# Two chained transformer blocks in one kernel: FFN products with the tokens stationary, 1/rms moved behind the products, token tiles staggered across stage borders

## The chip, the cores and the metric

The kernel runs on one core of a Trainium2 chip. The metric is the device time of one execution in microseconds, median over repeated runs. A profile is taken from one execution; its span runs from the first to the last instruction. Engines: PE (TensorE, matmul), PEld (its weight load), DVE (VectorE), ACT (ScalarE), POOL (GpSimd), SP (SyncE, here the queue that issues most DMAs).

## What is computed

The input is `x` of 256 tokens by 1024, in float32. Two layers of a first block and two of a second act on it. A block of the first kind is, per layer,

```python
h = rms_norm(x, ffn1_norm[l])
x = x + 0.5 * swiglu(h, ffn1_w_gate[l], ffn1_w_up[l], ffn1_w_down[l])
h = rms_norm(x, mix_norm[l])
... = split_in_proj(h @ w_in[l])       # four attentions side by side, 16 heads
x = x + o @ w_out[l]
h = rms_norm(x, ffn2_norm[l])
x = x + 0.5 * swiglu(h, ffn2_w_gate[l], ffn2_w_up[l], ffn2_w_down[l])
```

with `rms_norm(x, g) = x * rsqrt(mean(x*x) + eps) * g` and `swiglu(h, wg, wu, wd) = (silu(h @ wg) * (h @ wu)) @ wd`, 2816 hidden columns. A block of the second kind scales and shifts each normed input by rows that come from a 1024-vector `c` (`mod = silu(c) @ w_ada[l] + b_ada[l]`), mixes, norms the mixer's and the FFN's output again (`x + gate * rmsnorm(y, g_post)`), and has one FFN per layer.

```python
h = rmsnorm(x, g_ffn_pre[l]) * (1.0 + scale_f) + shift_f
x = x + gate_f * rmsnorm(swiglu_2(h, w_gate_up[l], w_down[l]), g_ffn_post[l])
```

## The kernel before

**Stages.** `STAGES` lists ten: f0 a0 f1 f2 a1 f3 b0 f4 b1 f5 (f an FFN, a a mixer of the first block, b one of the second). All engines go through them in the same order, each in its own program; semaphores are the only ties. X (256 x 1024) stays in SBUF as two token tiles t = 0, 1 of 128 partitions.

**Split products.** All large products are float32 made of two reduced parts: each operand is a high half (a rounded copy, tiles `Wh`, `Hh`, `PTh`) and a low half, the remainder (`Wl`, `Hl`, `PTl`). A product is three matmuls, high x high, high x low, low x high (`three`, lines 404 to 406; in the FFN lines 474 to 476).

**Weights.** They come as pieces of 128 x 1024 (512 KB) in the order of use: SP loads into six `raw` tiles, ACT writes the high half (line 791), DVE the remainder (line 1088), into rings of six `Wh` and `Wl`. In the programs `hi_to(n)` and `lo_to(n)` say how far the conversion goes at that point; ACT then waits in line for the raw tile and for the ring slot (`w_used`).

**Norm.** At each stage's start, `norm` in four programs: ACT squares X and sums (line 800); POOL takes the power -1/2 (lines 1554, 1556); PE turns X by eight transposes of 128 x 128 per tile (line 421) and spreads 1/rms over the partitions by small matmuls (line 426); DVE multiplies turned X, gain and 1/rms into `HT` (a part of `WK`, line 1132), ACT writes `Hh` (line 808 or 810) and DVE `Hl` (line 1124 or 1126), chunk by chunk of 128 columns of the model width, both tiles together.

**FFN** (`ffn`). For each of 22 groups f of 128 hidden columns: the gate and up weights are the stationary side, the turned tokens `Hh`, `Hl` move, 256 columns; 48 matmuls. ACT takes silu (line 827), DVE the product with up (line 1162), ACT and DVE split it (lines 831, 1164) into `PTh`, `PTl`, which already lie with hidden columns on partitions. The down product of group f - 1 follows: `PTh` stationary, the down weights move, 512 columns, 12 matmuls, accumulating in PSUM banks 0 to 3 over the whole stage. In f0 to f3 DVE also makes the rows of `w_ada` ("ada steps", line 1152, fed by ACT's DMAs into `BT`), with a small matmul, a row addition and a DMA out per eight steps.

**Mixers.** `project` has the tokens stationary and 512 weight columns moving (lines 404 to 406). Mixer a follows `walk_a`, which weaves projections, head norms, rotations, transposes and the 20 attention items; mixer b has 16 items. `out_proj` takes the eight output pieces one by one, both token tiles with each.

**Stage end.** `residual` on DVE (line 1192) adds the four banks to X, first tile 0, then tile 1; in stages b0 to f5 `post_norm` does it with squares on ACT (line 1050), POOL's power and two wide DVE operations (lines 1201, 1205). Then `norm` of the next stage begins.

## Time and profile before

| | us |
|---|---|
| median of 3 runs | 1968.66 (1967.34 to 1969.95) |
| the profiled execution's own time | 1968.9 |
| its span | 1967.0 |
| PE busy | 1752.2 (89% of the span) |
| DVE busy | 1292.5 (66%) |
| ACT busy | 900.1 (46%) |
| POOL busy | 105.8 (5%) |

The page counts 27994 instructions, 10912 of them matmuls. Busy time of PE is read with care: matmuls overlap, so the start-to-start distance in the timeline says what one costs in a stream. "Granted clock" is TensorE's clock as a share of its full speed.

### The profile page before, as it was taken

To read this page: it belongs to the slowest core of one execution; us is meant where nothing else is said; L and a number is where in the kernel's file an instruction comes from. 1 tells how busy PE (TensorE), PEld (TensorE's weight loads), DVE (VectorE), ACT (ScalarE), POOL (GpSimd) and SP (SyncE) were. 2 spreads that over 40 slices of the span, in tenths; PEclk is the share of its full clock that TensorE was granted. 3 is DMA by queue.
4 is the path that set the end of the run, shared out by engine and by line. 5 is a ranking of instruction groups with operands and counts; after the bars stand their busy time and mean duration, and the time that the engine had idled before them with its cause. 6 is when DMAs were issued, how large, how long until landed. Compare 5 with 4: busy or idle time off the path is not lost.

```text
span 1967.0 us, 27994 instructions
## 1 busy us (share of the span) xinstructions
PE 1752.2 (89%) x10912; PEld 1577.7 (80%) x10912; DVE 1292.5 (66%) x2143; ACT 900.1 (46%) x1577; POOL 105.8 (5%) x141
## 2 busy tenths in 40 slices
PE   6999976789999999986689999977899987779998
PEld 5999765579998999865579998866799976669997
DVE  5776668667776777668757776585555556754554
ACT  4444534444444444544434445464444455634443
POOL 0000012000000000011100000011000000200000
PEclk9999987699999999988589999968899988779999
DMA  7777522047775877632137875403355652134552
GB/s 266 263 258 233 203 90 82 22 158 251 261 240 183 270 264 239 211 107 77 31 118 250 273 247 174 147 1 118 140 184 183 182 162 81 63 105 155 191 182 89
DMA packets 99698, 332.01 MB, mean 169 GB/s; under 512 B 18624, under 2 KB 18880, under 8 KB 99056
## 3 DMA queue, kind: packets, MB, share of 16 engines
q1 hardware_dynamic: 84928, 277.84, 42.9%
q10 hardware_dynamic: 14640, 52.39, 7.6%
q8 instruction: 87, 1.43, 0.3%
q14 instruction: 43, 0.35, 0.1%
HBM read 329.09 MB, written 1.10 MB: 168 GB/s over the span
## 4 chain that ended last, share of the span: by engine, by line
PE 76%; DVE 13%; ACT 5%; issue 3%; POOL 2%; DMA 1%; ACTq 0%; DVEq 0%; POOLq 0%
PE PS L474 13%; PE PS L475 13%; PE PS L476 13%; PE PS L404 10%; PE PS L405 10%; PE PS L406 10%; DVE Wl L1088 2%; ACT Wh L791 1%; ACT WK L860 1%; PE PS L547 1%; DVE st L1222 1%; DVE WK L1219 1%; PE PS L528 1%; POOL A L1587 1%; PE PS L662 1%
## 5 line engine op out<-in xcount | busy, mean ns | idle before, releaser
L1088 DVE TENSOR_TENSOR Wl<-raw,Wh 128x1024 fp32r<-128x1024 f32 (+2 forms) x514 | 605.1, 1217 | 234.5 <-ACT Wh L791 233.7
L474 PE MATMUL PS<-Hh,Wh 128*128 128x256 f32 x2112 | 605.7, 287 | 14.1 <-DVE Hl L1124 9.0
L475 PE MATMUL PS<-Hl,Wh 128*128 128x256 f32 x2112 | 601.4, 285 | 0.0
L476 PE MATMUL PS<-Hh,Wl 128*128 128x256 f32 x2112 | 600.9, 285 | 0.0
L791 ACT ACTIVATE Wh<-raw 128x1024 fp32r<-128x1024 f32 (+2 forms) x514 | 509.1, 1036 | 113.5 <-DVE GQ L1174 61.2
L474 PEld LDWEIGHTS PS<-Hh,Wh 128*128 128x128 f32 x2112 | 407.5, 193 | 23.9 <-DVE WK L1132 14.7
L475 PEld LDWEIGHTS PS<-Hl,Wh 128*128 128x128 f32 x2112 | 409.1, 194 | 4.7
L476 PEld LDWEIGHTS PS<-Hh,Wl 128*128 128x128 f32 x2112 | 408.9, 194 | 0.0
L827 ACT ACTIVATE WK<-PS 128x256 f32<-128x256 f32 x132 | 50.7, 384 | 446.8 <-PE PS L476 446.8
L404 PE MATMUL PS<-Wh,Hh 128*128 128x512 f32 (+2 forms) x472 | 194.3, 412 | 24.3 <-DVE Hl L1474 6.2
L404 PE MATMUL PS<-Wh,PTh 128*128 128x512 f32 x528 | 207.2, 392 | 0.0
L405 PE MATMUL PS<-Wl,PTh 128*128 128x512 f32 x528 | 207.1, 392 | 0.0
L406 PE MATMUL PS<-Wh,PTl 128*128 128x512 f32 x528 | 205.3, 389 | 0.0
L405 PE MATMUL PS<-Wl,Hh 128*128 128x512 f32 (+2 forms) x472 | 190.2, 403 | 0.0
L406 PE MATMUL PS<-Wh,Hl 128*128 128x512 f32 (+2 forms) x472 | 188.9, 400 | 0.0
L1162 DVE TENSOR_TENSOR WK<-WK,PS 128x256 f32<-128x256 f32 x132 | 55.2, 419 | 189.0 <-ACT WK L827 188.5
L1152 DVE SCALAR_TENSOR_TENSOR GQ<-BT,cact,GQ 128x512 f32<-128x512 f32 x168 | 126.1, 751 | 21.7 <-DMA BT<-in_ada 14.6
L404 PEld LDWEIGHTS PS<-Wh,Hh 128*128 128x128 f32 x472 | 96.9, 205 | 47.1 <-issue 27.1
L406 PEld LDWEIGHTS PS<-Wh,PTl 128*128 128x128 f32 x528 | 99.2, 188 | 21.9
L404 PEld LDWEIGHTS PS<-Wh,PTh 128*128 128x128 f32 x528 | 99.5, 189 | 18.7
L547 PE MATMUL PS<-CT,WK 128*128 128x128 f32 x224 | 53.3, 363 | 68.2 <-POOL WK L1570 40.7
L405 PEld LDWEIGHTS PS<-Wl,PTh 128*128 128x128 f32 x528 | 99.5, 188 | 16.9
(191 smaller groups left out, 1872.3 us busy)
## 6 DMA issues: line engine op xcount, KB each, us to landing
raw<-in_ffn SPq DMA_DIRECT2D x396, 512.0 KB, 4.6
BT<-in_ada ACTq DMA_DIRECT2D x96, 512.0 KB, 4.4
raw<-in_win SPq DMA_DIRECT2D x64, 512.0 KB, 4.5
raw<-in_wo SPq DMA_DIRECT2D x32, 512.0 KB, 4.0
raw<-in_win SPq DMA_DIRECT2D x8, 420.0 KB, 4.0
BT<-in_nab SPq DMA_DIRECT2D x2, 1024.0 KB, 9.5
...
```

What stands on the lines that cost most here:

```text
L404: e.matmul(out_, xh, wh, start=start, stop=False)
L405: e.matmul(out_, xh, wl, start=False, stop=False)
L406: return e.matmul(out_, xl, wh, start=False, stop=stop)
L474: e.matmul(o, h[:, cc], Hh[:, c, :], start=c == 0, stop=False)
L475: e.matmul(o, h[:, cc], Hl[:, c, :], start=False, stop=False)
L476: ins = e.matmul(o, lo[:, cc], Hh[:, c, :], start=False, stop=c == 7)
L547: ins = e.transpose(PS[:, 5 + z % 2, col:col + 128], src, ident)
L791: e.activation(Wh[p % RING][:, 0:w], raw[p % RAW][:, 0:w], ACT.Copy).then_inc(w_hi, 1)
L827: e.activation(SB[:, f % 2, 0, :], PS[:, 4 + f % 2, 0:S], ACT.Silu).then_inc(f_silu, 1)
L1088: e.tensor_tensor(Wl[p % RING][:, 0:w], raw[p % RAW][:, 0:w], Wh[p % RING][:, 0:w].bitcast(f32), ALU.subtract).then_inc(w_lo, 1)
L1152: e.scalar_tensor_tensor(out=acc, in0=w, scalar=cact[:, c:c + 1], in1=acc, op0=ALU.mult, op1=ALU.add).then_inc(ada_step, 1)
L1162: e.tensor_tensor(SB[:, f % 2, 1, :], SB[:, f % 2, 0, :], PS[:, 4 + f % 2, S:2 * S], ALU.mult).then_inc(f_mul, 1)
```

## The change

**FFN.** A group is now 256 hidden columns (`NG` = 11), one token tile at a time. The turned tokens are the stationary side and a piece of gate and up weights moves: 256 gate and 256 up columns side by side, 512 in one PSUM bank (`gate_up`, banks 4 and 5 in turn). The host lays the weights out to match. The product `silu(gate) * up` then has tokens on partitions (`FA`, three buffers in `WK`), so PE turns it (`turn`, two transposes per group and tile, banks 6 and 7, shared with the ada rows) before ACT and DVE split it into `ATh`, `ATl` (four buffers in the memory of `PTh`, `PTl`). `down` is as before, per tile.

**1/rms.** In stages f0 to f3, a0 and a1 X is turned unscaled; the gain rides on the copy out of PSUM, and 1/rms (`rms(s, t)`, per token, which is now a partition) rides on the silu, the up product and the copies of the projections. In b and later FFNs a shift has to be added, so DVE first scales X by 1/rms into a spare tile (`scale_x`). The spreading matmuls are gone. ACT copies half of the turned chunks into `XT` and DVE the other half, 128 x 128 each, before the split.

**Order.** One function `walk(s)` gives each stage's events in order, and all engines follow it. `("gu", g, t, 0)` is gate/up of group g for tile t, `("down", g, t, chunks)`, `("turn", g, t, 0)` as above, `("res", s, t, 0)` the residual and the squares of tile t, `("turn_x", s, t, h)` the turning and splitting of half h of tile t for stage s, `("xs", ...)` the scaling. Tile 0 ends its stage early and is turned for the next one (`nxt`) while tile 1 still has products; tile 1 is turned (`mid`) after the next stage's first products of tile 0. `out_proj` gives its last pieces tile by tile.

**Weights.** Four more slots lie in the memory of `QTh`, `QTl` in FFNs and around them (`MORE`). `last_use`, `freed` and `slot_free` say when a piece's slot is free; `weights(s, i)` stands ahead of every event on ACT and DVE and converts up to `weights_to[s, i]`: what the event needs, plus at most `LIMIT` pieces whose slot is already free.

```diff
-NF = F // 128
+NG = F // 256
-RAW, RING = 6, 6
+RAW, RING, MORE = 6, 6, 4
+def walk(s):
+    kind, k = STAGES[s]
+    late = s >= 6
+    mid = [("turn_x", s, 1, 0), ("turn_x", s, 1, 1)]
+    nxt = [("turn_x", s + 1, 0, 0), ("turn_x", s + 1, 0, 1)] if s + 1 < len(STAGES) else [None, None]
+    scale = [[("xs", s + 1, t, 0)] if s + 1 in range(6, len(STAGES)) else [] for t in range(2)]
+    nlate = s + 1 >= 6
+    ev = []
+    if s == 0:
+        ev += [("turn_x", 0, t, h) for t in range(2) for h in range(2)]
+    if kind == "f":
+        def round_(g):
+            got = [("gu", g, 0, 0)]
+            if g:
+                got += [("turn", g - 1, 1, 0), ("down", g - 1, 0, (0, 1))]
+            got += [("gu", g, 1, 0), ("turn", g, 0, 0)]
+            if g:
+                got += [("down", g - 1, 1, (0, 1))]
+            return got
+        if s == 0:
+            ev += round_(0) + round_(1)
+        else:
+            ev += [("gu", 0, 0, 0), *(() if late else mid), ("gu", 1, 0, 0), *(mid if late else ()), ("gu", 0, 1, 0),
+                   ("turn", 0, 0, 0), ("gu", 1, 1, 0), ("turn", 0, 1, 0), ("down", 0, 0, (0, 1)), ("turn", 1, 0, 0),
+                   ("down", 0, 1, (0, 1))]
+        for g in range(2, NG - 2):
+            ev += round_(g)
+        y, z = NG - 2, NG - 1
+        ev += [("gu", y, 0, 0), ("turn", y - 1, 1, 0), ("down", y - 1, 0, (0, 1)), ("gu", z, 0, 0), ("turn", y, 0, 0),
+               ("down", y - 1, 1, (0, 1)), ("gu", y, 1, 0), ("turn", z, 0, 0), ("down", y, 0, (0, 1)), ("down", z, 0, (0, 1)),
+               ("turn", y, 1, 0), ("res", s, 0, 0), ("gu", z, 1, 0), *scale[0]]
+        if nlate:
+            ev += [("down", y, 1, (0,)), ("turn", z, 1, 0), ("down", y, 1, (1,)), ("down", z, 1, (0, 1)), *nxt]
+        else:
+            ev += [nxt[0], ("down", y, 1, (0,)), ("turn", z, 1, 0), ("down", y, 1, (1,)), nxt[1], ("down", z, 1, (0, 1))]
+    elif kind == "a":
+        ev += [("proj", 0, 0, 0), *mid, ("proj", 1, 0, 0), ("proj", 0, 1, 0), ("norm", 0, 0, 0), ("proj", 1, 1, 0), ("rope", 0, 0, 0),
...
+               *(("att", i, 0, 0) for i in range(10, ITEMS["a"] + 3)), ("mix", 0, 0, 0),
+               ("wo", (0,), 0, 0), ("wo", (0,), 1, 0), ("sums", 0, 0, 0), ("wo", (1,), 0, 0), ("wo", (1,), 1, 0),
+               ("wo", (2,), 0, 0), ("wo", (2,), 1, 0), ("rows", 0, 0, 0), ("wo", (3,), 0, 0), ("wo", (3,), 1, 0),
+               ("wo", (4,), 0, 0), ("wo", (4,), 1, 0), ("wo", (5, 6, 7), 0, 0), ("res", s, 0, 0), *scale[0],
+               ("wo", (5, 6), 1, 0), nxt[0], ("wo", (7,), 1, 0), nxt[1]]
+    else:
+        ev += [("proj", 0, 0, 0), ("proj", 1, 0, 0), *mid, ("proj", 0, 1, 0), ("proj", 1, 1, 0), ("proj", 2, 0, 0), ("proj", 2, 1, 0),
+               ("bulk", 0, 0, 0), ("proj", 3, 0, 0), ("proj", 3, 1, 0), ("lat", 0, 0, 0),
+               *(("att", i, 0, 0) for i in range(-1, ITEMS["b"] + 3)), ("mix", 0, 0, 0),
+               ("wo", (0,), 0, 0), ("wo", (0,), 1, 0), ("wo", (1,), 0, 0), ("wo", (1,), 1, 0),
+               ("wo", (2, 3, 4, 5, 6, 7), 0, 0), ("res", s, 0, 0), *scale[0], ("wo", (2, 3, 4, 5, 6, 7), 1, 0), *nxt]
+    ev += [("res", s, 1, 0), *scale[1]]
+    return [e for e in ev if e]
...
+        for p in range(NP):
+            s = stage_of[p]
+            wide = STAGES[s][0] == "f" or p < first[STAGES[s]] + 8
+            if p == first[STAGES[s]] and s and STAGES[s - 1][0] != "f":
+                for n in range(RING, RING + MORE):
+                    holder[n] = freed[wo_at[STAGES[s - 1]]] + 1
+            slots = range(RING + MORE if wide else RING)
+            slot_of[p] = min(slots, key=lambda n: (holder.get(n, 0), n))
+            slot_free[p] = holder.get(slot_of[p], 0)
+            holder[slot_of[p]] = freed[p] + 1
...
+        LIMIT = {"gu": 2, "turn": 1, "down": 2, "proj": 2, "att": 1, "wo": 2, "turn_x": 1, "mix": 2, "res": 1, "bulk": 2}
+        weights_to, n = {}, 0
+        for s in range(len(STAGES)):
+            for i, ev in enumerate(WALK[s]):
+                top = n
+                while top < min(NP, n + LIMIT.get(ev[0], 0)) and slot_free[top] <= freed_before[s, i]:
+                    top += 1
+                n = max([top, *(p + 1 for p in pieces_of(s, ev))])
+                weights_to[s, i] = n
...
...
+            def turn_x(s, t, h):
+                if h == 0:
...
+                    elif s < 6:
+                        e.wait_ge(x_ok, 2 * s - 1 + t)
+                    else:
+                        e.wait_ge(n_xs, 2 * (s - 6) + t + 1)
+                src = X[:, t, :] if s < 6 else scaled_x(s, t)
+                for c in range(4):
+                    ins = e.transpose(PS[:, 2 * t + h, c * 128:c * 128 + 128], src[:, (4 * h + c) * 128:(4 * h + c) * 128 + 128], ident)
+                ins.then_inc(n_turn, 1)
...
+            def gate_up(s, i, k, g, t):
+                n = gu_no[k, g, t]
+                if n >= 2:
+                    e.wait_ge(f_mul, n - 1)
+                q = slice(t * 128, t * 128 + 128)
+                for m in range(4):
+                    p = ffn_at[k, "gu", g] + m
                     e.wait_ge(w_lo, p + 1)
...
+                        ins = three(PS[:, 4 + n % 2, :], Hh[:, c, q], Hl[:, c, q], h[:, cc], lo[:, cc], c == 0, c == 7)
-                            e.matmul(o, h[:, cc], Hh[:, c, :], start=c == 0, stop=False)
-                            e.matmul(o, h[:, cc], Hl[:, c, :], start=False, stop=False)
-                            ins = e.matmul(o, lo[:, cc], Hh[:, c, :], start=False, stop=c == 7)
...
+            def turn(k, g, t):
+                z, n = ring_no[k, g, t], gu_no[k, g, t]
+                if z >= 2:
+                    e.wait_ge(f_z, z - 1)
+                e.wait_ge(f_mul, n + 1)
+                for c in range(2):
+                    ins = e.transpose(PS[:, 6 + z % 2, c * 128:c * 128 + 128], FA[:, n % 3, 1, c * 128:c * 128 + 128], ident)
+                ins.then_inc(f_turn, 1)
+            def down(s, i, k, g, t, chunks):
+                n, z = turn_no[k, g, t] % 4, ring_no[k, g, t]
+                e.wait_ge(f_z, z + 1)
+                for x in chunks:
+                    e.wait_ge(w_lo, ffn_at[k, "down", g] + x + 1)
+                last = g == NG - 1
+                for j, x in ([(j, x) for j in range(2) for x in chunks] if last else [(j, x) for x in chunks for j in range(2)]):
+                    p = ffn_at[k, "down", g] + x
+                    cc = slice(512 * j, 512 * j + 512)
+                    q = slice(x * 128, x * 128 + 128)
+                    ins = three(PS[:, 2 * t + j, :], ATh[:, n, q], ATl[:, n, q], high(p)[:, cc], low(p)[:, cc],
+                                g == 0 and x == 0, last and x == 1)
...
+            def out_proj(s, i, stage, chunks, t, ready):
+                q = slice(t * 128, t * 128 + 128)
+                for j, c in ([(j, c) for j in range(2) for c in chunks] if 7 in chunks else [(j, c) for c in chunks for j in range(2)]):
                     p = wo_at[stage] + c
+                    if j == 0 and t == 0:
+                        e.wait_ge(w_lo, p + 1)
+                        ready(c)
+                    cc = slice(j * 512, j * 512 + 512)
+                    ins = three(PS[:, 2 * t + j, :], Hh[:, c, q], Hl[:, c, q], high(p)[:, cc], low(p)[:, cc], c == 0, c == 7)
...
```

In `act_program` (ScalarE):

```diff
+            def weights(s, i):
+                while state["hi"] < weights_to[s, i]:
...
+            def turn_x(s, t, h):
+                scale, shift = columns_of(s)
+                o, q = 16 * s + 8 * t, slice(t * 128, t * 128 + 128)
+                if h == 0:
...
+                    e.wait_ge(n_turn, 4 * s + 2 * t + 1)
+                    if o:
+                        e.wait_ge(n_lo, o)
+                    for c in range(4):
+                        src = PS[:, 2 * t, c * 128:c * 128 + 128]
+                        if shift is None:
+                            ins = e.activation(XT[:, c, :], src, ACT.Copy, scale=scale[:, c:c + 1])
+                        else:
+                            ins = e.activation(XT[:, c, :], src, ACT.Identity, scale=scale[:, c:c + 1], bias=shift[:, c:c + 1])
+                        ins.then_inc(n_ya, 1)
...
+            def gate(s, i, k, g, t):
...
+                    ins = e.activation(FA[:, n % 3, 0, :], PS[:, 4 + n % 2, 0:256], ACT.Silu, scale=rms(s, t))
...
+            def turn(k, g, t):
+                n, z = turn_no[k, g, t], ring_no[k, g, t]
+                e.wait_ge(f_turn, n + 1)
+                e.activation(ATh[:, n % 4, :], PS[:, 6 + z % 2, 0:256], ACT.Copy).then_inc(f_hi, 1)
...
```

In `dve_program` (VectorE):

```diff
+            def scale_x(s, t):
+                e.wait_ge(n_rs, 2 * s + t + 1)
+                e.tensor_scalar(scaled_x(s, t), X[:, t, :], rms(s, t), None, ALU.mult).then_inc(n_xs, 1)
+            def turn_x(s, t, h):
+                scale, shift = columns_of(s)
+                o, q = 16 * s + 8 * t, slice(t * 128, t * 128 + 128)
+                if h:
...
+                    e.wait_ge(n_turn, 4 * s + 2 * t + 2)
+                    if o:
+                        e.wait_ge(n_lo, o)
+                    for c in range(4, 8):
+                        src = PS[:, 2 * t + 1, (c - 4) * 128:(c - 4) * 128 + 128]
+                        if shift is None:
+                            ins = e.tensor_scalar(XT[:, c, :], src, scale[:, c:c + 1], None, ALU.mult)
+                        else:
+                            ins = e.tensor_scalar(XT[:, c, :], src, scale[:, c:c + 1], shift[:, c:c + 1], ALU.mult, ALU.add)
+                        ins.then_inc(n_yd, 1)
+                for c in range(4 * h, 4 * h + 4):
+                    e.wait_ge(n_hi, o + c + 1)
+                    e.tensor_tensor(Hl[:, c, q], XT[:, c, :], Hh[:, c, q].bitcast(f32), ALU.subtract).then_inc(n_lo, 1)
...
+            def product(s, k, g, t):
+                n, f = gu_no[k, g, t], gu_in[k, g, t]
+                if k < 4:
+                    ada_steps(k, f)
+                e.wait_ge(f_silu, n + 1)
+                up = PS[:, 4 + n % 2, 256:512]
+                if s < 6:
+                    ins = e.scalar_tensor_tensor(out=FA[:, n % 3, 1, :], in0=up, scalar=rms(s, t), in1=FA[:, n % 3, 0, :],
+                                                 op0=ALU.mult, op1=ALU.mult)
+                else:
+                    ins = e.tensor_tensor(FA[:, n % 3, 1, :], FA[:, n % 3, 0, :], up, ALU.mult)
...
+            def turn(k, g, t):
+                n, z = turn_no[k, g, t], ring_no[k, g, t]
+                e.wait_ge(f_hi, n + 1)
+                e.tensor_tensor(ATl[:, n % 4, :], PS[:, 6 + z % 2, 0:256], ATh[:, n % 4, :].bitcast(f32),
...
```

In `sp_program` (SyncE):

```diff
+                    e.wait_ge(n_turn, 4 * (norm_no["b", l] + 1))
                     e.dma_start(BT[:, :, :, :], d["t5b"]).then_inc(bt_in, 16)
```

## Rows read from the trace of the kernel before

**Rows 1.** The page: totals, granted clock in 40 slices (tenths), chain that ended last by engine.

```profile
span 1967.0 us, 27994 instructions
...
PE 1752.2 (89%) x10912; PEld 1577.7 (80%) x10912; DVE 1292.5 (66%) x2143; ACT 900.1 (46%) x1577; POOL 105.8 (5%) x141
...
PEclk9999987699999999988589999968899988779999
...
PE 76%; DVE 13%; ACT 5%; issue 3%; POOL 2%; DMA 1%; ACTq 0%; DVEq 0%; POOLq 0%
```

**Rows 2.** Busy us per engine by stretch (x count); then granted clock, DMA share, GB/s.

```profile
60.00:162.00 102.00, 102.00 (x714) 95.68 (x713) 77.87 (x99) 46.06 (x64) 0.00 (x0) 1.00 0.79 268
222.00:411.00 189.00, 148.53 (x710) 118.83 (x710) 136.87 (x316) 85.63 (x195) 24.73 (x20) 0.80 0.25 80
```

**Rows 3.** Timeline of PE in the first FFN: start us, us, engine, line, tiles, count.

```profile
63.64 0.40 PE L404 MATMUL PS<-Wh,PTh 128*128 128x512 f32 x1
...
66.39 0.28 PE L474 MATMUL PS<-Hh,Wh 128*128 128x256 f32 x1
...
72.14 0.40 PE L404 MATMUL PS<-Wh,PTh 128*128 128x512 f32 x1
```

**Rows 4.** Timeline of PE at the first mixer-to-FFN border.

```profile
408.97 0.39 PE L404 MATMUL PS<-Wh,Hh 128*128 128x512 f32 x1
...
410.78 0.39 PE L406 MATMUL PS<-Wh,Hl 128*128 128x512 f32 x1
414.83 1.10 PE L421 MATMUL PS<-CT,X 128*128 128x128 f32 x8 [3.67 <-DVE X L1192]
...
421.86 0.36 PE L474 MATMUL PS<-Hh,Wh 128*128 128x256 f32 x1 [1.99 <-DVE Hl L1124]
...
435.87 0.40 PE L404 MATMUL PS<-Wh,PTh 128*128 128x512 f32 x1
```

**Rows 5.** Timeline of PE at three other borders.

```profile
215.75 0.39 PE L406 MATMUL PS<-Wh,PTl 128*128 128x512 f32 x1
...
222.57 0.47 PE L404 MATMUL PS<-Wh,Hh 128*128 128x512 f32 x1 [2.21 <-DVE Hl L1124]
...
1378.18 0.39 PE L406 MATMUL PS<-Wh,Hl 128*128 128x512 f32 x1
1384.32 1.97 PE L421 MATMUL PS<-CT,X 128*128 128x128 f32 x8 [5.75 <-DVE X L1205]
...
1392.53 0.55 PE L474 MATMUL PS<-Hh,Wh 128*128 128x256 f32 x1 [2.15 <-DVE Hl L1126]
...
1582.16 0.39 PE L406 MATMUL PS<-Wh,PTl 128*128 128x512 f32 x1
...
1594.09 0.77 PE L404 MATMUL PS<-Wh,Hh 128*128 128x512 f32 x1 [2.15 <-DVE Hl L1126]
```

**Rows 6.** Instructions by line, shapes apart: out<-in, count, busy us, mean ns, idle before.

```profile
L1088 DVE TENSOR_TENSOR Wl<-raw,Wh 128x1024 fp32r<-128x1024 f32 x494 | 588.2, 1231 | 220.3 <-ACT Wh L791 219.5
L791 ACT ACTIVATE Wh<-raw 128x1024 fp32r<-128x1024 f32 x494 | 494.4, 1046 | 110.9 <-DVE GQ L1174 61.2 <-PE PS L406 48.4 <-issue 1.0
...
L1152 DVE SCALAR_TENSOR_TENSOR GQ<-BT,cact,GQ 128x512 f32<-128x512 f32 x168 | 126.1, 751 | 21.7 <-DMA BT<-in_ada 14.6
...
L831 ACT ACTIVATE PTh<-WK 128x256 fp32r<-128x256 f32 x132 | 55.1, 418 | 109.4 <-DVE WK L1162 109.4
...
L1132 DVE SCALAR_TENSOR_TENSOR WK<-PS,SM,R 128x256 f32<-128x256 f32 x48 | 22.5, 480 | 11.8 <-ACT R L804 11.8
...
L1238 DVE TENSOR_SCALAR WK<-WK,st 128x128 f32<-128x128 f32 x16 | 4.6, 287 | 0.6
...
L886 ACT ACTIVATE Hh<-PS 64x128 fp32r<-64x128 f32 x16 | 4.3, 267 | 0.1
```

**Rows 7.** Timeline of ACT at the start.

```profile
17.71 2.93 ACT L791 ACTIVATE Wh<-raw 128x1024 fp32r<-128x1024 f32 x3
```

**Rows 8.** Who waited for whom: us in total, times, longest.

```profile
ACT Wh L791 <- PE PS L406: 51.0, 38, 4.9
```

1272 lines of the change are left out of this document (635 added, 637 removed).

## The prediction, made before the changed kernel ran

> **What bounds the kernel now.** I read the page's totals first, then busy time by stretch, then single matmuls in order of time, last each border between stages. The totals show PE busy 89% of a 1967.0 us span, with a granted clock that dips only in some slices, and a chain of waits that is 76% PE [rows 1]. An average over unlike stages says little, so: inside an FFN, PE is busy for the whole stretch at full clock, DVE for 76% of it, and DMA moves 268 GB/s; in the first mixer PE is busy 79% at clock 0.80 and DVE 72% [rows 2]. So an FFN is bound by how fast PE starts products and nothing else; a mixer waits in many small places. In steady FFN work 48 products of 256 columns take 66.39 to 72.14 us, 0.120 us each; 12 products of 512 columns take 63.64 to 66.39, 0.229 each [rows 3]. In the output projection 512 columns with an activation as the stationary side start every 0.227 us (408.97 to 410.78, eight of them) [rows 4]. I use 0.228. The width, not the side that stands still, sets the price.
>
> The third place is the border. From the last product of the mixer to the first of the FFN (410.78+0.23 to 421.86) PE has no product for 10.9 us: it waits for the residual, then turns X (eight transposes in 1.10 us, so (1.10-0.27)/7, about 0.118 each when warm), then waits for rms and the scaled halves [rows 4]. It comes back cold: the 96 products before the first down product take 14.0 us (421.86 to 435.87) where 96 x 0.120 is 11.5, a further 2.5. The other kinds: after an FFN with a plain residual 6.6 us (215.75+0.23 to 222.57), after a late mixer 14.1 (1378.18+0.23 to 1392.53), after a late FFN 11.7 (1582.16+0.23 to 1594.09) [rows 5].
>
> **FFN products.** Removed: 6336 gate/up products of 256 columns, 6336 x 0.120 = 760. Added: 3168 of 512, 3168 x 0.228 = 722. Gain 37 (36.7 with the unrounded 0.1198). Added too: the product a comes out with tokens on partitions and must be turned, 11 groups x 2 tiles x 2 x 6 stages = 264 transposes. At 0.118 that is 31.2; the cold rate (1.97 us for eight, 0.22 each [rows 5]) would make it 59, and I take the warm one because the stretch is warm. Net gain 5.5; bounds -22 and +8 (transposes at 0.11). The down products keep form and number.
>
> One rule of the Trainium skill speaks against this. "TensorE: Matmul & The Clock Gate", Back-to-back issue gap, puts a warm matmul at 262 cycles for 256 columns and 518 for 512, so one of 512 saves 2.5 ns on two of 256; by it the products gain 8 us, not 37, and the sum ends 29 us later, near 1958. The trace disagrees (0.240 against 0.228) and I follow it.
>
> Do the other engines keep up? Per group of 256 hidden columns PE has 72 products and 4 transposes, 72 x 0.228 + 0.5 = 16.9 us. DVE has six weight remainders at 1.231, two products at 0.48, two remainders of a at 0.42 and up to eight ada steps at 0.751: 7.4+1.0+0.8+6.0 = 15.2, plus a row of ada; ACT has six halves at 1.046 and little else [rows 6]. Tight in rounds with eight steps, but products are asked for one half-round (8.2 us) after they can be made and weights a round after. I cost it at nothing; if the cover went, some 30 rounds with ada would pay up to 1 us each.
>
> At each FFN's end pieces of the last two groups compete for slots. Following the planner's rule through the diff, the last down piece comes after ACT's silu for gate/up(9,1), one weight half and one high half of a, and then needs its own half and remainder: 0.4+1.0+0.4+1.0+1.2, 4.3 us with the hand-overs, while PE asks for it after a pair of transposes and 12 products, 3.0 us: 1.3 late in each of six FFNs, -7.8 (bounds 0 and -12).
>
> **Borders.** The staggering leaves tile 1's last products as cover for tile 0's residual, turning and split. But both ACT and DVE work through their queues in the order of the walk, and `weights(s, i)` stands ahead of each event. That matters more than the cover's length. All 16 transposes stay, 1.9 us a border.
>
> After an FFN with plain residual (a0, f2, a1): measured from the end of gate/up(10,1), ACT does the silu (0.4), one weight half, four scaled copies and four halves of turned X (about 0.27 each, between the 0.267 of 64x128 on ACT and the 0.287 of 128x128 on DVE [rows 6]), then three weight halves at the 0.98 that three in a row take [rows 7], and only then the high half of turned a: at 6.8. DVE follows with the third weight remainder and a's at 8.4. PE has reached down(10,1) at 3.9 and waits 4.5. Then X's second half is ready in time. Cost 4.5 + 1.9 + 0.3 = 6.7 against 6.6 plus the cold start (2.5 for an FFN; I take half, 1.3, for a mixer). Three of them: 24.9 before, 20.1 after, gain 4.8.
>
> After an early mixer (f1, f3): nothing like `turn` stands between; residual, squares and one weight half end 3.0 us after tile 0's last output product, the first half of X is split by 5.0 when the last output product ends, but the second half waits behind two weight remainders and four scalings on DVE, until 11.1, while PE needs it at 7.8: 3.3 + 1.9 + 0.3 = 5.5 against 10.9 + 2.5. Gain 15.8 for two.
>
> FFN to b0: down(10,1) waits 3.0 behind four weight pieces, X's first pieces 1.5, the second tile, which has no product between its turning and its use, about 2: 8.5 with the transposes, against 6.6 + 1.3. Gain -0.6. FFN to b1: the same 9.0 (post-norm fits under gate/up(10,1)), against 11.7 + 1.3. Gain 4.0.
>
> Late mixer to f4, f5: the cover is 36 products, 8.2 us; tile 0's chain is the 5.9 us seen from the last product to its first transpose (1378.41 to 1384.32 [rows 5]) plus squares, power and the new scaling of x, 3.2 more, so 9.1, and ACT and DVE have three weight pieces in it: first product at about 13, that is 4.8 late; second half 1.2; second tile 0.9 + 2. Together 8.9 against 14.1 + 2.5. Gain 15.4 for two.
>
> Sum of borders 39.4. Bounds: if nothing queued ahead mattered, 106 (88 of gaps and 18 of cold starts) less 9 x 1.9 and some 11 of late exposure, 78; if each of some 30 weight pieces queued there took a further 0.9 us, because raw data or a slot is late, 12.
>
> **The rest.** The start: X can be turned at once, but ACT must deliver four wide pieces (three took 2.93 us [rows 7]) between 24 small copies before the first group is done: -2. The end: only tile 1's norm is left, +1. Mixers: the same attention; conversions wait for a slot freed beforehand instead of blocking ACT on PE (51.0 us of such waits [rows 8]), but the last piece of each projection comes one event later: +4, bounds -10 and +14. 1/rms rides on copies that exist already, 0. Table t5b now waits on SP for the turned X and holds up the piece behind it; a projection pair (11 us) covers it, 0.
>
> **Sum.** 5.5 - 7.8 + 39.4 - 2 + 1 + 4 = 40.1 off the profiled execution's 1968.9 (span 1967.0 [rows 1], 1.9 around it): 1928.8. The median of the runs is 1968.66, 0.2 lower, so 1929.
>
> **Rivals.** (A) Order in the queues costs nothing: raw pieces are there and ACT, idle most of an FFN, runs ahead. Borders gain 78, the FFN end loses nothing: 1968.9 - 78 - 5.5 + 2 - 1 - 4 = 1882. For it: DVE idles 24% in FFNs. Against: it idles between tasks, not at the border.
>
> (B) The border gives nearly everything back: 12 for borders, -10 for mixers: 1968.9 - 5.5 + 7.8 - 12 + 2 - 1 + 10 = 1970 at worst, 1950 with half of each. For it: weight conversions already stand on the mixers' waits.
>
> (C) Slower. Turning a inside the product stream is the mechanism: PE is in order, so if a pair of transposes waits for gate, product and DVE's queue, the whole FFN pays. There are 132 pairs; the kernel gets slower once each costs 0.30 us more than 0.24. At 0.5 it is 66: 1995. Against: each pair stands at least 8.2 us behind its gate/up products, and the chain is some 2.2 us long.
> The Trainium skill has a rule in this direction ("TensorE: Matmul & The Clock Gate", Part 4: PE-mode transpose): about 275 ns for a transpose inside a kernel. By that the 264 cost 41 us more and the time is 1970, no change. The warm rows here give 0.118 and the cold 0.22; the trace does not agree.
>
> **Chances.** Forecast 0.55, A 0.20, B 0.18, C 0.07. A measurement tells 0.2%, 4 us, from no change. Faster: all of forecast and A, most of B, 0.92; same 0.03 (from B); slower 0.05. The range 1886 to 1954 leaves out half of A, B's worst end and C; the forecast's own is 1910 to 1945.
>
> **What would show it.** PE starts of 512-column gate/up products every 0.227 to 0.229 us and pairs of transposes near 0.24 with no idle before them; PE busy without a gap in groups 2 to 8 of each FFN; an idle of 3 to 5 us before down(10,1) of the first five FFNs, released by the remainder of turned a, with weight remainders just ahead of it on DVE; about 3 us before X's second half after a0 and a1; 5 us at the first product of f4 and f5. Wrong: no idle at down(10,1) (then A), idle at turned a inside the groups (C), or PE waiting for weight remainders in an FFN's middle.

## The result, and the profile after

The changed kernel takes 1990.5 us (median of four runs, 1986.2 to 1994.7) against 1968.0 beside it: ratio 1.0113, with a 95% interval of 1.0089 to 1.0136. It is 1.1% slower, where 1929 was forecast. A second set of runs gave 1990.3 (1.0112, interval 1.0097 to 1.0127).

The page of the changed kernel, to be held against [rows 1]:

```profile
span 1989.1 us, 22440 instructions
...
PE 1734.6 (87%) x7968; PEld 1419.9 (71%) x7968; DVE 1283.5 (65%) x2231; ACT 914.6 (46%) x1727; POOL 102.9 (5%) x141
...
PEclk9999988599999999998589999968899998778999
...
PE 56%; DVE 23%; ACT 9%; DMA 5%; issue 5%; POOL 1%; ACTq 0%; SPq 0%; DVEq 0%; POOLq 0%
```

PE is busy for 18 us less and the span is 22 us longer, so some 40 us of waiting came in. The chain that ended last was 76% PE and is now 56%: DVE has 10 points more, ACT and DMA 4 each, issue 2. Busy time by stretch (columns as in [rows 2], an FFN and the first mixer):

```profile
60.00:162.00 102.00, 100.18 (x450) 81.95 (x449) 76.67 (x101) 42.54 (x61) 0.00 (x0) 1.00 0.75 262
225.20:422.70 197.50, 151.70 (x728) 121.24 (x727) 136.57 (x321) 89.41 (x211) 26.27 (x24) 0.80 0.25 80
```

The FFN is no longer gapless, at the same full clock. The mixer, from its first product to the next stage's, takes 197.5 us for the same attention where it took 199.3 (222.57 to 421.86, [rows 4, 5]), although the idle time at its far end is gone: its interior became longer. The products themselves do what was forecast. PE in an FFN's middle, to be held against [rows 3]:

```profile
101.28 0.39 PE L561 MATMUL PS<-Wh,Hl 128*128 128x512 f32 x1
101.51 0.38 PE L620 MATMUL PS<-CT,WK 128*128 128x128 f32 x2
101.64 0.48 PE L559 MATMUL PS<-QTh,PTh 128*128 128x512 f32 x1
101.96 0.39 PE L560 MATMUL PS<-QTl,PTh 128*128 128x512 f32 x1
102.19 0.40 PE L561 MATMUL PS<-QTh,PTl 128*128 128x512 f32 x1
```

Products start every 0.227 to 0.23 us. From the start of a turning pair to the start of the second product behind it (101.51 to 101.96) are 0.45 us where 0.23 would be without the pair, so a pair costs 0.22 us.

Who PE waits for (us in total, times, longest):

```profile
PE PS L700 <- POOL WK L1791: 56.3, 32, 3.1
PE PS L559 <- DVE Hl L1334: 42.1, 11, 11.5
PE PS L559 <- DVE Wl L1284: 30.5, 19, 3.0
PE PS L559 <- DVE PTl L1381: 26.5, 16, 4.3
```

The third kind, a weight remainder that is late, is among no waits of PE in the kernel before. To place the loss I summed, over every stretch, the distance between the starts of successive matmuls less the "warm distance" of their kind, which is the distance that they keep in an undisturbed stream (0.2275 us for 512 columns, 0.1198 for 256, 0.109 for a transpose). What is left is waiting, and products that run slower than that. A border is from 12 us of such work before a stage's first product to 20 us behind it; an interior is what lies between two borders, and that of f0 begins with its first product. These figures scatter between executions: single FFNs and mixers by up to some 4 us, and a second execution of the changed kernel reads 35.7 for the six FFN interiors, 74.7 for the borders and 1 less for the mixers.

| us over warm distance | before | changed | four edits | best |
|---|---|---|---|---|
| borders a0 / f2 / a1 | 4.8 / 6.7 / 6.0 | 6.8 / 7.0 / 6.7 | 6.2 / 6.2 / 6.2 | 2.8 / 3.0 / 2.9 |
| borders f1 / f3 | 11.2 / 11.2 | 2.4 / 4.0 | 2.4 / 4.0 | 2.4 / 2.4 |
| borders b0 / b1 | 6.3 / 11.2 | 8.5 / 9.0 | 9.3 / 8.8 | 10.2 / 10.8 |
| borders f4 / f5 | 14.8 / 14.8 | 16.2 / 16.0 | 8.0 / 8.1 | 8.1 / 8.1 |
| all nine borders | 86.9 | 76.7 | 59.2 | 50.7 |
| six FFN interiors | 5.2 | 31.5 | 20.0 | 20.1 |
| four mixer interiors | 234 | 258 | 242 | 236 |
| all matmuls at warm distance | 1610.2 | 1596.3 | 1596.3 | 1596.3 |

"Four edits" and "best" (the one with 1932.4 us) are kernels of the experiments below.

### The profile page after: what moved, and what is told of

It reads as the page before. It is cut to its first block, busy times and chain, and to the rows that moved or that the text cites. A ratio compares the mean times of both kernels' runs of the same rounds, so it can differ in the third digit from the quotient of the medians.

```text
span 1989.1 us, 22440 instructions
## 1 busy us (share of the span) xinstructions
PE 1734.6 (87%) x7968; PEld 1419.9 (71%) x7968; DVE 1283.5 (65%) x2231; ACT 914.6 (46%) x1727; POOL 102.9 (5%) x141
## 4 chain that ended last, share of the span: by engine, by line
PE 56%; DVE 23%; ACT 9%; DMA 5%; issue 5%; POOL 1%; ACTq 0%; SPq 0%; DVEq 0%; POOLq 0%
PE PS L559 17%; PE PS L561 17%; PE PS L560 17%; DVE Wl L1284 6%; DMA BT<-in_ada 4%; DVE QTl L1284 3%; ACT Wh L952 3%; DVE GQ L1350 3%; ACT QTh L952 1%; DVE st L1426 1%; DVE WK L1423 1%; ACT WK L1041 1%; DMA raw<-in_ffn 1%; PE PS L681 1%; PE PS L620 1%
## 5 line engine op out<-in xcount | busy, mean ns | idle before, releaser
L1284 DVE TENSOR_TENSOR Wl<-raw,Wh 128x1024 fp32r<-128x1024 f32 (+2 forms) x340 | 402.7, 1212 | 161.3 <-ACT Wh L952 160.5
L559 PE MATMUL PS<-Wh,Hh 128*128 128x512 f32 (+2 forms) x1032 | 411.6, 399 | 57.3 <-DVE Wl L1284 27.0
L560 PE MATMUL PS<-Wl,Hh 128*128 128x512 f32 (+2 forms) x1032 | 404.8, 392 | 0.0
L561 PE MATMUL PS<-Wh,Hl 128*128 128x512 f32 (+2 forms) x1032 | 404.0, 391 | 0.0
L559 PEld LDWEIGHTS PS<-Wh,Hh 128*128 128x128 f32 x1032 | 199.7, 193 | 105.8 <-DVE Wl L1284 45.3
L1284 DVE TENSOR_TENSOR QTl<-raw,QTh 128x1024 fp32r<-128x1024 f32 x174 | 207.8, 1219 | 36.0 <-ACT QTh L952 35.9
L561 PEld LDWEIGHTS PS<-Wh,Hl 128*128 128x128 f32 x1032 | 199.3, 193 | 39.9
L560 PEld LDWEIGHTS PS<-Wl,Hh 128*128 128x128 f32 x1032 | 199.9, 194 | 37.4
L559 PE MATMUL PS<-QTh,Hh 128*128 128x512 f32 x496 | 197.7, 399 | 23.4 <-DVE Hl L1334 23.4
L560 PE MATMUL PS<-QTl,Hh 128*128 128x512 f32 x496 | 196.9, 397 | 0.0
L561 PE MATMUL PS<-QTh,Hl 128*128 128x512 f32 x496 | 196.8, 397 | 0.0
L1350 DVE SCALAR_TENSOR_TENSOR GQ<-BT,cact,GQ 128x512 f32<-128x512 f32 x168 | 126.1, 750 | 64.2 <-DMA BT<-in_ada 57.9
L561 PEld LDWEIGHTS PS<-QTh,Hl 128*128 128x128 f32 x496 | 95.4, 192 | 20.3
```

Source lines behind the costliest of these rows:

```text
L559: e.matmul(out_, xh, wh, start=start, stop=False)
L560: e.matmul(out_, xh, wl, start=False, stop=False)
L561: return e.matmul(out_, xl, wh, start=False, stop=stop)
L1284: e.tensor_tensor(low(p)[:, 0:w], raw[p % RAW][:, 0:w], high(p)[:, 0:w].bitcast(f32), ALU.subtract).then_inc(w_lo, 1)
L1350: e.scalar_tensor_tensor(out=acc, in0=w, scalar=cact[:, c:c + 1], in1=acc, op0=ALU.mult, op1=ALU.add).then_inc(ada_step, 1)
```

## The experiments

Times below are medians of four to ten runs, each with its 95% interval; "the changed kernel" is 1990.5. The ratios are against the kernel before in the same set of runs. A profile is of one execution, which can lie some us off the median.

### A gate load on SP, ahead of the weights

In the changed kernel's border b0 to f4, PE (first two lines), then ACT, then who SP waits for:

```profile
1411.44 0.50 PE L559 MATMUL PS<-Wh,Hh 128*128 128x512 f32 x1 [1.64 <-DVE Wl L1284]
...
1421.98 0.77 PE L559 MATMUL PS<-QTh,Hh 128*128 128x512 f32 x1 [8.02 <-DVE Hl L1334]
```

```profile
1415.94 1.06 ACT L952 ACTIVATE Wh<-raw 128x1024 fp32r<-128x1024 f32 x1 [6.44 <-DMA raw<-in_ffn]
```

```profile
SPq L541 <- DVE X L1409: 46.8, 2, 23.4
```

PE's releaser is `Hl`, the split X of token tile 1. But ACT, which writes its high half, was waiting for a raw weight in its queue, and that load stood at SP behind a gate load, which waited 23.4 us for x_ok, the semaphore that counts the residuals done (the hook `gate_f`). The wait names both tiles of stage b, and tile 1's now ends inside the FFN. The kernel before has the same wait. There it lasts 16.3 us and the gate load goes out at 1386.74, 5.8 us ahead of f4's first product (1392.53, [rows 5]); in the changed kernel it goes out at 1407.40, 9.0 us behind it (1398.40). First the kernel before, then the changed one:

```profile
SPq L386 <- DVE X L1205: 32.5, 2, 16.3
...
1386.74 0.33 SPq L386 DMA_DIRECT2D GQ<-mod_scratch  x1
```

```profile
1407.40 0.33 SPq L541 DMA_DIRECT2D GQ<-mod_scratch  x1
```

```diff
-                hooks[first["f", 4 + l] + 8] = ("gate_f", l)
+                hooks[first["f", 4 + l] + 20] = ("gate_f", l)
```

> In the changed kernel SP waits for x_ok of both token tiles of stage b before it loads f4's (f5's) post-norm gate, at the eighth weight piece of the stage, and every later weight load stands behind that wait in SP's queue. With the tiles staggered the second tile's x_ok comes only after the FFN's first products have begun. This kernel moves that gate load behind the twentieth piece and changes nothing else. Theory (the wait on SP makes the weights late): the ACT wait of 6.4 us for a raw weight piece near 1416 us goes, the idle 8.0 us (f4) and 7.0 us (f5) of PE at the second tile's first products shrink to 1 or 2 us, the clock stays up there, and the time is 12 to 16 us below the changed kernel: 1975 to 1979 us. Rival (the second tile's turning and its gates on ACT and DVE are late in any case): PE idles at least 6 us at both places and the time is 1987 to 1991 us.

1981.6 us, ratio 1.0066 (1.0051 to 1.0081): 8.9 below the changed kernel, 3 less than the theory's least. The place answers to the theory; the SP wait at L541 for X is gone and PE at tile 1's first product of f4 shows:

```profile
1423.37 0.47 PE L559 MATMUL PS<-QTh,Hh 128*128 128x512 f32 x1 [1.78 <-DVE Hl L1334]
```

8.02 became 1.78, f5's 7.05 also 1.78, and both borders fell from 16 to 8 us: 6.2 us of it is the shorter idle time of f4, most of the rest that the products behind it no longer start 0.43 us apart. Of these 16 us only 9 came out in the total: the other stretches read 6 us more in this execution, each within its scatter. That the gate load's place costs time, and at which border, is shown; the size in the total is known to some 5 us.

### The last pieces of a projection's weights

PE in the changed kernel's a0:

```profile
276.11 0.80 PE L559 MATMUL PS<-Wh,Hh 128*128 128x512 f32 x1 [2.44 <-DVE Wl L1284]
296.23 0.50 PE L559 MATMUL PS<-Wh,Hh 128*128 128x512 f32 x1 [1.74 <-DVE Wl L1284]
300.88 0.50 PE L559 MATMUL PS<-Wh,Hh 128*128 128x512 f32 x1 [2.99 <-DVE Wl L1284]
324.87 0.38 PE L559 MATMUL PS<-Wh,Hh 128*128 128x256 f32 x1 [2.32 <-DVE Wl L1284]
```

9.5 us in a0 and 10.4 in a1. The planner lets a piece be converted only where its slot was free before the event, so the last ones are converted at the very event that needs them.

```diff
                 while top < min(NP, n + LIMIT.get(ev[0], 0)) and slot_free[top] <= freed_before[s, i]:
                     top += 1
+                if ev[0] == "proj" and ev[2] == 1:
+                    block = first[STAGES[s]] + 4 * ev[1] + 8
+                    while top < block and slot_free[top] <= freed_before[s, i] + 2:
+                        top += 1
```

> The changed kernel converts a weight piece only at an event before which its slot is already free; the kernel before let ACT wait inside a projection's second product for the slots that this same product frees. Here the second product of each projection converts the next projection's pieces that way again; all else is as in the changed kernel. Theory (the last pieces of each projection are late): the 30.5 us that PE waits for DVE's weight halves (19 waits, up to 3.0 us) fall below 12 us, the two a stages are 7 to 10 us shorter each, and the time is 14 to 20 us below the changed kernel: 1971 to 1977 us. Rival (the attention's own chain through ACT, DVE and POOL sets the a stages, so what is saved at the projections comes back as waits in the attention): waits for weights fall, waits of L700 and L770 grow, and the time is 1985 to 1991 us.

1974.0 us, ratio 1.0024 (1.0007 to 1.0040): 16.5 below. Interiors of a0 and a1: 75.6 to 68.1 and 73.9 to 68.4, close to what they were before the change (68.1, 67.3). PE's waits for weights:

```profile
PE PS L563 <- DVE Wl L1288: 9.6, 9, 1.6
```

The theory holds. ACT blocked on PE for a slot ([rows 8], 51.0 us) was not waste: it bought weights one event early.

### The end of the FFN

```diff
-            ev += [nxt[0], ("down", y, 1, (0,)), ("turn", z, 1, 0), ("down", y, 1, (1,)), nxt[1], ("down", z, 1, (0, 1))]
+            ev += [("down", y, 1, (0,)), ("turn", z, 1, 0), nxt[0], ("down", y, 1, (1,)), nxt[1], ("down", z, 1, (0, 1))]
...
+                hold = STAGES[s][0] == "f" and (ev[:3] == ("turn", NG - 1, 1) or ev == ("down", NG - 2, 1, (0,)))
-                while top < min(NP, n + LIMIT.get(ev[0], 0)) and slot_free[top] <= freed_before[s, i]:
+                while top < min(NP, n + (0 if hold else LIMIT.get(ev[0], 0))) and slot_free[top] <= freed_before[s, i]:
```

> At the FFN's end the changed kernel has, between the last gate and up product and the turning of its result, the next stage's first turning of X and up to three weight conversions on ACT and DVE. Here the turning of X stands behind the turning of the result (in f0 to f3), and no weights are converted at the two events before it (all six FFNs). Theory (these operations stand in the way of the last activation): PE's idle time before the last down product falls from 4.3 us (f0, f1, f2), 2.5 (f3) and 2.8 (f4) to at most 1.5 us each; some 1 us each comes back where the next stage's first product waits for the turned X; the time is 8 to 13 us below the changed kernel: 1978 to 1983 us. Rival (what is gained at the last down product is lost in full at the border, since ACT and DVE have the same work either way): first products of the next stages start as late after the last down product's end as now plus 3 us, and the time is 1988 to 1992 us.

1984.4 us, ratio 1.0099 (1.0060 to 1.0137): 6.1 below, and between the two. At f0's end PE idled 4.29 us in the changed kernel, and behind that ten products started 0.43 us apart (granted clock 0.53 from 219.83 to 224.80). With the edit it does not idle there, but 1.31 us for X's second half and 2.76 for tile 1's residual:

```profile
219.83 0.79 PE L559 MATMUL PS<-Wh,PTh 128*128 128x512 f32 x1 [4.29 <-DVE PTl L1381]
220.42 0.63 PE L560 MATMUL PS<-Wl,PTh 128*128 128x512 f32 x1
220.85 0.63 PE L561 MATMUL PS<-Wh,PTl 128*128 128x512 f32 x1
```

```profile
223.88 0.47 PE L560 MATMUL PS<-QTh,Hh 128*128 128x512 f32 x1 [1.31 <-DVE Hl L1335]
...
229.61 1.09 PE L577 MATMUL PS<-CT,X 128*128 128x128 f32 x8 [2.76 <-DVE X L1397]
```

The held-back conversions now stand on DVE ahead of tile 1's residual (three remainders from 224.86 to 228.36, the residual at 228.28). So the halves were run apart, the first line of the diff alone (g1) and the rest alone (g2), beside a repeat of the changed kernel (1990.3).

> The changed kernel once more, as the base of the two that follow: 1986 to 1995 us.

> The changed kernel with the first half of the edit at the FFN's end alone: the turning of the next stage's X stands behind the turning of the last activation in f0 to f3, and weights are converted where they were. Theory (the turning of X on ACT and DVE is the larger part of what stands in the way of the last activation): PE's idle 4.3 us before the last down product falls to 2 to 3 us in f0 to f2; f3 (2.5 us) loses at most 1 us; f4 (2.8 us) is unchanged; the time is 2 to 6 us below the changed kernel. Rival (the three conversions alone are the cause): the idle stays above 3.5 us in f0 to f2.

> The changed kernel with the other half alone: no weights are converted at the two events before the last turning, and the turning of X stays ahead of it. Theory (the conversions are the smaller part): the idle before the last down product falls from 4.3 to 2 to 3 us in f0 to f2, from 2.8 to below 1 us in f4; the time is 2 to 6 us below the changed kernel. Rival (the turning of X alone is the cause): 4 us or more stay in f0 to f2, and only f4 gains.

g1: 1981.4 us, ratio 1.0070 (1.0055 to 1.0086), 8.9 below the repeat; the idle is 1.52 in f0, f1 and f2, and the slow products behind it are gone too, which its theory did not count (borders a0, f2, a1: 8.7 instead of 20.5). g2: 1984.0, ratio 1.0081 (1.0060 to 1.0102), 6.3 below: the idle is 0.21, but PE waits 2.6 us for tile 1's residual a few products later. Each half alone gains more than its theory said, and together they gain no more than one. The intervals of g1, g2 and the whole edit overlap, so these runs do not say which half to keep; h1 below does, the turning of X ahead of the turned activation was the step to undo.

### The density of the adaLN steps

```diff
-    n = min(max(n - 2, 0), 15)
-    return 16 * (n // 5) + (0, 3, 6, 8, 12)[n % 5]
+    n = min(max(n - 1, 0), 18)
+    return 8 * (n // 3) + (0, 3, 6)[n % 3]
```

> The first four FFNs also compute the adaLN rows on DVE: 48 steps each, in the changed kernel spread over 15 gate-and-up events as 3, 3, 2, 4, 4 steps, with two buffers for the loads; a row of 4 steps uses up both buffers, and the next steps wait up to 3.6 us for a load. Here they are spread over 18 events as 3, 3, 2 steps, as the kernel before had them. Theory (the density of the steps makes DVE wait for loads, and PE for DVE): DVE's wait for these loads falls from 57.9 us to below 35 us, the interior of f0 to f3 loses 3 to 5 us each, and the time is 10 to 18 us below the changed kernel: 1973 to 1981 us. Rival (the load is late whatever the spread, because ACT issues it behind a gate that waits for PE): DVE waits as long, the waits come at more events, and the time is 1987 to 1995 us.

> The changed kernel with all but the first two of the 24 adaLN weight loads of each of the first four FFNs left out; the DVE steps all run, on the buffers' old contents. It tells the wait for the load from the cost of the steps. Theory (it is the load of up to two 512 KB units between two rounds that makes DVE, and then PE, late): DVE's wait for these loads (57.9 us) falls below 6 us, the interiors of f0 to f3 come 3 to 5 us each nearer to full speed, and the time is 10 to 18 us below the changed kernel: 1973 to 1981 us. Rival (the steps themselves, up to four of 0.6 us ahead of the product on DVE, make PE late): the interiors fall by less than 1.5 us each and the time is 1985 to 1991 us.

Even spread: 1976.1 us, ratio 1.0039 (1.0028 to 1.0050), 14.4 below. The kernel that leaves the loads out, and so computes other adaLN rows: 1977.5, ratio 1.0057 (1.0039 to 1.0075), 13.0 below. The interiors of f0 to f3 fall from 27.9 (32.1 in the changed kernel's second execution) to 16.6 and to 15.0. The second of these was read in the slowest of ten runs, 1989.5 us, whose borders and mixers together read 11 us above the changed kernel's. Both times came as the theory had them, and without the loads the wait for them is gone as it said. But with the even spread DVE waits longer for its loads (first fence the changed kernel, second the even spread), and yet the kernel is faster. So the length of that wait does not tell what it costs. What fell is ACT's wait for DVE's steps:

```profile
DVE GQ L1350 <- DMA BT<-in_ada: 57.9, 27, 4.0
...
ACT Vh L1014 <- DVE GQ L1350: 90.7, 23, 6.8
```

```profile
DVE GQ L1350 <- DMA BT<-in_ada: 76.3, 36, 4.7
...
ACT Vh L1014 <- DVE GQ L1350: 17.1, 20, 2.4
```

L1014 is ACT's high half of an accumulated row. It needs the eighth step, and behind it in ACT's queue stand weight halves and the turned activation. One such place in the changed kernel, DVE and ACT:

```profile
505.52 1.54 DVE L1350 SCALAR_TENSOR_TENSOR GQ<-BT,cact,GQ 128x512 f32<-128x512 f32 x2 [3.55 <-DMA BT<-in_ada]
507.09 0.63 ACT L1014 ACTIVATE Vh<-GQ 128x512 fp32r<-128x512 f32 x1 [3.56 <-DVE GQ L1350]
```

To tell it from the order within DVE's queue, the steps were put behind the product, their number and loads unchanged:

```diff
-                if k < 4:
-                    ada_steps(k, f)
                 e.wait_ge(f_silu, n + 1)
...
                 ins.then_inc(f_mul, 1)
                 if k < 4:
+                    ada_steps(k, f)
                     for x in range(6 * k + ada_to(f) // 8, 6 * k + ada_to(f + 1) // 8):
```

> The changed kernel with the adaLN steps of each event behind the product on DVE instead of ahead of it; their number per event and the loads stay. Theory (the product and the turning of its result wait behind a step that waits for its load): the product no longer waits, PE's idle time for PTl in f0 to f3 falls, the interiors of f0 to f3 lose 2 to 4 us each, and the time is 8 to 15 us below the changed kernel: 1975 to 1982 us. Rival (the steps' wait stands ahead of the turning and of the conversions as much as ahead of the product, so that the order within an event gives nothing): 1987 to 1993 us.

2007.5 us, ratio 1.0200 (1.0184 to 1.0216): 17 slower, against theory and rival. DVE's wait for loads is down to 18.1 us; ACT's waits behind the steps are the longest of these kernels:

```profile
ACT Vh L1014 <- DVE GQ L1350: 99.5, 24, 7.0
...
ACT Wh L952 <- DVE GQ L1373: 59.5, 13, 7.5
...
ACT QTh L952 <- DVE GQ L1373: 42.2, 9, 6.6
```

ACT's waits for the adaLN work of DVE, all kinds, sum to 201 us here (the three above), 167 in the changed kernel, 88 without the loads, 75 with the even spread and 61 before. The time of the four kernels that carry the change (2007, 1990, 1977, 1976) follows that sum and not DVE's own wait, in order though not in proportion; the last two cannot be told apart. That the spread of the steps costs these 14 us is shown. That the copy at L1014 is what passes the delay to PE is read from the profiles and not shown; a kernel with this copy one event later was not tried.

### All four, and the attention's conversions

> The four edits together: the gate load behind the twentieth piece, the next projection's pieces converted inside a projection's second product, the FFN's last activation ahead of the next turning of X and of conversions, the adaLN steps spread over 18 events. Alone they stood 8.9, 16.5, 6.1 and 14.4 us below the changed kernel's 1990.5 us. Theory (four separate places, each bound by PE's own queue): the gains add to 46 us, and the time is 1940 to 1950 us, below the kernel before (1968.7). Rival (the edits free each other's idle time, so that they overlap, or their medians carry some us of scatter each): half the sum, 1962 to 1970 us.

1944.1 us, ratio 0.9879 (0.9860 to 0.9899). The four gains sum to 45.9, measured are 46.4: they add, as far as medians with some us of scatter each can tell.

```diff
+                kd, lim = STAGES[s][0], LIMIT.get(ev[0], 0)
+                if ev[0] == "att":
+                    lim = int(ev[1] >= 9 if kd == "a" else ev[1] >= 0 and ev[1] % 3 == 0)
```

> As the kernel with the four edits, and in the attention weight pieces are converted as the kernel before does it: in stage a from item 9 on alone, in stage b one piece every third item, instead of one at every event at which a slot is free. Theory (conversions on ACT and DVE stand in the way of the first attention items: PE's waits for POOL's probabilities, L700, are 56.3 us in the changed kernel and 40.7 us before): these waits fall by 8 us or more, and the time is 6 to 12 us below the kernel with the four edits. Rival (the waits for POOL come from the projections' new order, and the conversions moved to later items delay those instead): the waits stay within 4 us and the time within 4 us.

1942.4 us, ratio 0.9866 (0.9851 to 0.9881): the rival's "within 4 us"; PE's waits for POOL fall from 53.5 to 47.2 only. The interiors of b0 and b1 read 101.5 us instead of 105.8 (98.8 before the change, 108.7 with it), within what single executions scatter. But the four kernels with this edit read 101 to 103, and the staggered ones without it 104 to 112, so these conversions seem to cost the b mixers some us; in the time that is not shown.

### Without the staggering

```diff
-    late = s >= 6
+    late = False
...
-    nxt = [("turn_x", s + 1, 0, 0), ("turn_x", s + 1, 0, 1)] if s + 1 < len(STAGES) else [None, None]
+    nxt = [None, None]
...
-    ev = []
-    if s == 0:
-        ev += [("turn_x", 0, t, h) for t in range(2) for h in range(2)]
+    ev = [("turn_x", s, t, h) for t in range(2) for h in range(2)]
+    mid = []
```

> As the kernel with the four edits, but the token tiles are not staggered at the stage borders: both tiles of X are turned in one go at the start of each stage, behind the residual of both. The products, their order within the stage and the 1/rms on the products stay. It tells what the staggering itself gives. Theory (the staggering is worth much, and what the changed kernel lost lay elsewhere): each of the nine borders has PE idle 6 to 9 us and then below full clock, as the kernel before had (8 to 15 us over full speed), against some 4 to 8 us with the staggering: 15 to 45 us above the kernel with the four edits. Rival (DVE and ACT have the same chain of work at a border either way, and the staggering only moves the idle time): within 8 us of it.

1974.4 us, ratio 1.0030 (1.0017 to 1.0043): 30.3 above the kernel with the four edits. The nine borders sum to 92.6 us against 59.2. The staggering is worth some 30 us, once these four side effects are undone.

### Towards the best

g3 puts `mid` behind two products (`late = s >= 6 or s in (1, 3, 4)`, and `("proj", 1, 0, 0)` ahead of `*mid` in stage a). h1 takes the `hold` line out again and leaves all else as in f2; h3 is h1 with `mid` later for s in (1, 4).

> As the kernel with the four edits and the attention's conversions as before (1942.4 us), and at the borders to a0, f2 and a1 the second token tile of X is turned behind two products of the first tile (11 us) instead of one (5.5 us): there PE waited 2.8 us each for the residual of that tile. Theory (the residual, the turning and the splitting of a tile are one chain through DVE and ACT; a later turning only moves PE's idle time to the second tile's first product): the 2.8 us go, 2 to 4 us of waiting for the second tile's Hl come, and the time is within 4 us of 1942. Rival (the second product covers the residual and the rest is covered too): 6 to 9 us less, 1933 to 1937 us.

> As the kernel with the four edits and the attention's conversions as before (1942.4 us), but weights are converted at the FFN's end where the changed kernel does it. Theory (the held-back conversions all come at the border, ahead of the second tile's residual on DVE, where PE then waits 2.8 us for it in a0, f2 and a1): PE idles 1.5 us before the last down product and not for the residual; 0 to 4 us below 1942.4 us: 1937 to 1942. Rival (the 3 us between the two runs with one and both halves were scatter): the same idle time at another place, 1942 to 1946 us.

> As the kernel with the conversions kept, and the second tile's turning behind two products at the borders to a0 and a1 alone, where this gave 3 us together (at the border to f2 it cost 3.5 us: a wait of 5.0 us for Hl). Theory (the gains add): 1933 to 1938 us, the shortest of all. Rival (with the conversions kept there is no wait for the residual left that the later turning could cover): 1938 to 1943 us.

g3: 1937.9 us, ratio 0.9845 (0.9828 to 0.9861), 4.5 below f2, between theory and rival: less at a0 and a1, but 9.7 instead of 6.2 at f2, with a wait of 5.0 us for `Hl`. h1: 1932.4, ratio 0.9818 (0.9805 to 0.9832), 10.0 below f2 and more than its theory gave, from the `hold` line alone. With the conversions kept, PE at the end of f0 in h1 has two short waits:

```profile
214.62 0.50 PE L566 MATMUL PS<-Wh,PTh 128*128 128x512 f32 x1 [1.52 <-DVE PTl L1388]
...
223.82 1.09 PE L583 MATMUL PS<-CT,X 128*128 128x128 f32 x8 [0.46 <-DVE X L1403]
```

h3: 1934.1, ratio 0.9823 (0.9810 to 0.9836): with only 0.5 us of waiting for the residual left, the later turning adds nothing, as the rival says (its time was given from too high a base); h1 and h3 cannot be told apart. h1 is faster than the changed kernel and the kernel before, 1.8% below the latter. It keeps the change and undoes five of its side effects (the gate load's place, the late weights of the projections, the turning of X ahead of the last activation, the dense adaLN steps, the conversions in the attention), and in its FFN (60:162) PE is again busy throughout; its page's chain is back at 70% PE:

```profile
60.00:162.00 102.00, 102.00 (x461) 83.94 (x460) 76.24 (x99) 45.93 (x64) 0.00 (x0) 1.00 0.75 262
```

```profile
PE 70%; DVE 15%; ACT 8%; issue 4%; POOL 2%; DMA 1%; ACTq 0%; POOLq 0%; DVEq 0%
```

## Why the prediction was wrong, step by step

The forecast of -40 turned into +22: 62 us. In its own terms:

- **FFN products**, +5.5: right, and low. By the warm distances the products gain 38.3 and 132 turning pairs of 0.22 us cost 29.0, and all matmuls together are 13.9 shorter (among them the spreading of 1/rms, which the forecast left out). Eight us better than forecast. The rule of the Trainium skill that was weighed there ("TensorE: Matmul & The Clock Gate", Back-to-back issue gap) is not borne out by the trace after either: a product of 512 columns costs 0.2275 us, 12 ns less than two of 256 (0.2396), where the page's cycles, given there for an isolated matmul, make it 2.5 ns. Its 275 ns for a transpose (same page, Part 4: PE-mode transpose) is what one transpose shows here as its duration (median 271 ns in `turn`), but not what it costs in the stream: a pair costs 0.22 us. Rival C did not occur as priced. Its sign, PE idle inside the groups for the remainder of turned a, does show in f0 to f3, eleven times with 8.3 us in all; with the even spread it is three times with 3.4.
- **The FFN's end**, -7.8: right; PE idles 1.27 to 1.37 us there in six FFNs, 8.0.
- **The adaLN rounds**, "I cost it at nothing": wrong. The FFN interiors lost 26.3 (30.5 by the second execution) and not 7.8. The kernel with even spread and the one without loads each put 11 to 13 us of it on these rounds (interiors), and 13 to 14 in the time. Another 2.3 are waits behind the very first product. Some 4 are left; with the even spread a wait of 1.1 us before the first down product of f1, f2 and f3 is still there. The step summed DVE's busy time per group, 15.2 of 16.9 us, and looked at steps of 0.75 us. It did not ask who waits for the eighth step: ACT, in order, with weight halves behind it (as read from the profiles above). The bound named beside it, 30 rounds at up to 1 us, would have covered the size.
- **Borders after an early mixer**, 15.8: measured 16.0 (22.4 to 6.4). The wait forecast for X's second half is there, with 1.9 us where 3.3 stood; f3 has 1.6 us of slower products behind it, f1 none.
- **Borders a0, f2, a1**, 4.8: the hand-made queue was right, PE idles 4.29 us at each where 4.5 was forecast, but the sum is -3.0 (17.5 to 20.5). What failed is the cost put behind it, "Cost 4.5 + 1.9 + 0.3": the forecast charges cold starts to the kernel before and none to its own idle time. Behind the 4.29 us ten products start 0.43 us apart instead of 0.23, at a granted clock of 0.53, which is 2.3 us at each border. Less the transposes, which the table counts with the matmuls (16 x 0.109, 1.7 a border), the forecast comes to 14.9 for the three and 20.5 are measured: 5.6 of the 7.8 missed. The other 2.2 are cold starts credited to the kernel before (19.7 against 17.5): where the forecast says "I take half, 1.3, for a mixer", a0 has none (granted clock 1.00 from 222 to 230).
- **b0, b1**, -0.6 and 4.0: measured -2.2 and 2.2.
- **"Late mixer to f4, f5", 8.9 each**: the step that failed worst, 16.2 and 16.0, so -2.6 instead of +15.4. The list of what stood ahead at that border had the pieces on ACT and DVE, and left out SP's queue: its wait for tile 1's x_ok, with all later weights behind. The first experiment shows it; without it these borders come to 8.1, within 1 us of the hand-worked figure. That nearness is in part luck, since its parts differ: 2.3 us at f4's first product where 4.8 stood, 1.7 for a weight and 1.8 for tile 1, the rest slower products.
- **Mixers**, +4 with bounds -10 and +14: measured -24, outside the bounds. In a0 and a1 it is 14 us, "the last piece of each projection comes one event later", which I named and set below the gain from blocking less; the second experiment gives 13 of them back. The other 10 are in b0 and b1, where only 2 to 3 are left in the best kernel; no single cause was told apart there.
- **Start and end**, -2 and +1: about +4 together as booked here. The first product starts at 20.3 us and not at 23.7, and from the start of the last product to the end are 8.1 us instead of 9.2. The start's two waits for weights, 1.7 and 1.1 us, come after its first product and stand in f0's interior (2.3 us more than before), so the start gained 0.7 us by itself.

Sum of the misses: borders 29, mixers 28, FFN interiors 18, less 8 and 5: 62. Of the rivals, B ("the border gives nearly everything back") has the right manner and too small a loss. "PE waiting for weight remainders in an FFN's middle" was named as a sign of error; some of these waits are in FFNs, but two thirds (19.9 of 30.5 us) came in a0 and a1. The forecast's view of what the staggering itself is worth stands in the main: 30 us measured by taking it out of the kernel with the four edits, 39 forecast. In the changed kernel as it was, the borders gave 10.
